# Convolution transfers moved to GpSimd's queue, and gated linear attention slots dealt by product weight

## The reference, cut to what matters

```python
x = layer_norm(x, ln_in_g, ln_in_b)
gq, gk, gv, gr, glow, sq, sk, sv, cb, cc, ch = split_cols(x @ w_in)
go = gated_linear_attention(gq, gk, gv, gr, glow)      # recurrent, blocks of 64 tokens
so = stick_breaking_attention(sq, sk, sv)
co = cb * causal_conv3(cc * ch, conv_w)                # 256 channels
x = layer_norm(ALPHA * x + concat(go, so, co) @ w_out, ln1_g, ln1_b)
x = layer_norm(ALPHA * x + square(relu(x @ w_up)) @ w_down, ln2_g, ln2_b)
```

## Time and profile before

| what | value |
|---|---|
| median of 3 runs | 3136.07 us (3127.56 to 3136.89) |
| the profiled execution: its time, its span | 3133.53 us, 3131.8 us |
| PE busy, DVE busy, ACT busy, POOL busy | 88%, 48%, 34%, 9% of the span |
| mean granted clock of PE | 0.931 |
| `phase_head`, from the span's start to the barrier | 977 us |

### The profile page before, as it was taken

How to read it: one execution, slowest core, us unless ns; L and a number is a source line. 1 busy time by engine, 2 the same in 40 slices (tenths; PEclk the granted TensorE clock), 3 DMA queues, 4 the chain that set the end, 5 groups by cost and what they waited for, 6 DMA issues and landing times. The chain is left out here.

```text
span 3131.8 us, 40707 instructions
## 1 busy us (share of the span) xinstructions
PE 2756.6 (88%) x14670; PEld 2328.9 (74%) x14670; DVE 1501.9 (48%) x2346; ACT 1065.7 (34%) x1768; POOL 266.5 (9%) x285
## 2 busy tenths in 40 slices
PE   5989989899733367999999999999999988999997
PEld 4778787799722355888877888877888866888885
DVE  3446545643433546666556644445644424522224
ACT  1334333333212433444442434443434322322221
POOL 0030020200300001000001100001100000000000
PEclk9989999999855578999999999999999999999998
DMA  4635454343314754666665766665766554545452
GB/s 135 192 117 168 142 165 147 119 126 118 94 30 133 223 165 136 200 214 211 193 209 165 242 193 224 195 206 187 231 206 216 178 174 143 181 157 161 151 172 98
DMA packets 430004, 525.84 MB, mean 168 GB/s; under 512 B 31312, under 2 KB 305152, under 8 KB 429808
## 3 DMA queue, kind: packets, MB, share of 16 engines
q1 hardware_dynamic: 408592, 497.14, 50.2%
q10 hardware_dynamic: 21216, 26.10, 2.4%
HBM read 422.34 MB, written 100.80 MB: 167 GB/s over the span
## 5 line engine op out<-in xcount | busy, mean ns | idle before, releaser
L111 PE MATMUL p_ps_u<-p_xh,p_wh 128*128 128x512 f32 (+1 forms) x1280 | 453.4, 354 | 5.3 <-DVE p_xl L1614 5.3
L112 PE MATMUL p_ps_u<-p_xh,p_wl 128*128 128x512 f32 (+1 forms) x1280 | 451.9, 353 | 0.0
L113 PE MATMUL p_ps_u<-p_xl,p_wh 128*128 128x512 f32 (+1 forms) x1280 | 451.8, 353 | 0.0
L1563 DVE SCALAR_TENSOR_TENSOR p_res<-p_res,p_ps_d 128x512 f32<-128x512 f32 (+1 forms) x340 | 232.1, 685 | 451.4 <-PE p_ps_d L113 445.6
L111 PE MATMUL p_ps_d<-p_wh,p_hh 128*128 128x512 f32 (+1 forms) x1088 | 432.3, 397 | 15.4 <-DVE p_res L1563 13.2
L112 PE MATMUL p_ps_d<-p_wh,p_hl 128*128 128x512 f32 (+1 forms) x1088 | 428.5, 394 | 0.0
L113 PE MATMUL p_ps_d<-p_wl,p_hh 128*128 128x512 f32 (+1 forms) x1088 | 428.2, 394 | 0.0
L1472 ACT ACTIVATE p_wh<-p_wst 128x1024 fp32r<-128x1024 f32 x288 | 294.0, 1049 | 278.8 <-PE p_ps_d L113 219.6
L1621 DVE TENSOR_TENSOR p_r<-p_r 128x512 f32<-128x512 f32 (+1 forms) x160 | 95.8, 599 | 461.4 <-ACT p_hh L1502 461.2
L676 DVE TENSOR_TENSOR p_wl<-p_wst,p_wh 128x1024 fp32r<-128x1024 f32 x96 | 118.0, 1236 | 356.1 <-ACT p_wh L537 355.8
L1495 ACT ACTIVATE p_r<-p_ps_u 128x512 f32<-128x512 f32 (+1 forms) x160 | 83.8, 524 | 578.9 <-PE p_ps_u L113 578.9
(11 more groups left out here) (154 smaller groups left out, 4748.5 us busy)
## 6 DMA issues: line engine op xcount, KB each, us to landing
p_wl<-wlo_scratch SPq DMA_DIRECT2D x216, 512.0 KB, 5.2
p_wst<-in_w_up SPq DMA_DIRECT2D x128, 512.0 KB, 5.8
p_wst<-in_w_down SPq DMA_DIRECT2D x128, 512.0 KB, 5.0
p_wst<-in_w_in SPq DMA_DIRECT2D x96, 512.0 KB, 3.9
wlo_scratch<-p_wl SPq DMA_DIRECT2D x72, 512.0 KB, 3.5
p_kk<-ks_scratch SPq DMA_DIRECT2D x84, 256.0 KB, 5.8
p_vv<-vs_scratch SPq DMA_DIRECT2D x84, 256.0 KB, 4.5
p_wst<-in_w_out SPq DMA_DIRECT2D x32, 512.0 KB, 5.9
```

Of the source, the lines that this page charges most:

```text
L111: pe.matmul(out, lhs_hi, rhs_hi, start=first, stop=False, skip_group_check=skip)
L112: pe.matmul(out, lhs_lo, rhs_hi, start=False, stop=False, skip_group_check=skip)
L113: return pe.matmul(out, lhs_hi, rhs_lo, start=False, stop=last, skip_group_check=skip)
L1563: dve.scalar_tensor_tensor(out=acc, in0=acc, scalar=scale, in1=ps_d[:c, d % DB, :], op0=ALU.mult, op1=ALU.add).then_inc(d_free, 1)
```

## The change

Two things change, both in `phase_head`.

1. The convolution's transfers go from SP to POOL. `c_load` is no more; POOL itself waits for the stores, issues the three loads, does its arithmetic, waits for its own last result and issues the store and the state's transfers.
2. The slots are dealt by weight. From the first F 8 on, an F product counts 2 and a T product 1 (176 in all), and slots are taken so that their number keeps up with 132 times the share of the weight spent, at most two behind one product. Slots are now taken behind T products of all passes. An ahead slot may follow one product behind F 8 as before; a body waits for T pass 1 of its tokens. The two halves of an input normalisation (`norm_a`, `norm_b`) come behind successive F products from F 0 on.

By the new rule, worked from the diff, 16 slots are left for the drain (it begins with "intra 14, gate_sum 8"). Behind these products of the list come two slots: F 13, 15 of the first group; F 4, 6, 8, 10, 12, 14, 16 of the second; F 3, 5, 9, 10, 11, 12, 13, 15 of the third; F 9 to 16 and the first two T products of pass 2 in the last. Behind F 9 of the third and the last group come "load 4, gate 4" and "load 6, gate 6"; behind F 10 gate_sum and decay; behind F 11 level_mul and the first level product.

```diff
@@ the list
-                if step[0] == "F" or step[3] % 2 == 1:
-                    take_slot()
-                ready = [dense_at.get(("F", min(t // 512, 3), conv_f), len(dense_at)) for x, t, cnt in conv]
-                if conv_put < len(conv) and ready[conv_put] + 2 <= len(dense_at):
-                    order += [("c_load", conv_put), ("conv", conv_put)]
+                for n in range(2):
+                    if taken + n < n_slots * spent / sum(weight) and (n == 0 or taken + 1.5 < n_slots * spent / sum(weight)):
+                        taken += take_slot()
+                done.add(("F",) + step[2:4] if step[0] == "F" else ("T",) + step[2:4] if step[4] == len(gtiles[step[2]]) - 1 else None)
+                if conv_put < len(conv) and ("F", min(conv[conv_put][1] // 512, 3), conv_f) in done:
+                    order.append(("conv", conv_put))
...
+        n_slots = sum(len(x) for x in aheads) + 2 * len(bodies[-1]) + NG
+        opens = dense.index([x for x in dense if x[:4] == ("F", 0, 0, gla_f)][0]) + 1
+        weight = [{"F": 2, "T": 1}.get(x[0], 0) if i > opens else 0 for i, x in enumerate(dense)]
...
@@ take_slot
-            if body < NG and ag > body:
+            if b < NG and a > b and ("T", source(b), 1) in done:
...
@@ SP
-                elif what == "c_load":
...
-                elif what == "conv":
...
-                    sp.wait_ge(c_y, 6 * (k + 1))
-                    sp.dma_start(mixt_dram[768 + P * x:768 + P * x + P, t:t + cnt], cin[:, 1, :cnt]).then_inc(c_out, 16)
...
@@ POOL, in its conv step
+                    if x == 0:
+                        wait_stores(pool, results[("F", min(t // 512, 3), conv_f)])
+                    if k:
+                        pool.wait_ge(c_out, 16 * k)
+                    for n, z in enumerate((Z_CC, Z_CH, Z_CB)):
+                        pool.dma_start(cin[:, n, :cnt], zt_dram[z + P * x:z + P * x + P, t:t + cnt]).then_inc(c_in, 16)
...
+                    pool.wait_ge(c_y, 6 * k + 6)
+                    pool.dma_start(mixt_dram[768 + P * x:768 + P * x + P, t:t + cnt], y).then_inc(c_out, 16)
...
+            pool.wait_ge(cs_out, 64)
+            pool.wait_ge(c_out, 16 * len(conv))
```

More of the change, by code:

```diff
@@ L211, in weights, with t_steps @@
             return len(wunits) - 1
-        def t_steps(g, p):
+        def t_steps(sec, g, p):
             u = weights("T", pairs[p], 0)
             weights("T", pairs[p], 1)
[L216 to L230, removed]
-            else:
[L232 to L246, removed]
@@ new lines, in t_steps @@
+            return [("T", sec, g, p, ti, u) for ti in range(len(gtiles[g]))]
+        BOTH = ([0, 1], list(range(len(fs))), [2, 3])
+        sections = [(g, BOTH) for g in range(len(GROUPS))]
+        visits = []
+        for sec, (g, _) in enumerate(sections):
+            again = g in [x for x, _ in sections[:sec]]
+            visits += [dict(sec=sec, t=t, o=o, c=c, again=again) for t, o, c in gtiles[g]]
+        visit_no = {(vt["sec"], vt["t"]): i for i, vt in enumerate(visits)}
+        NORMS = len([vt for vt in visits if not vt["again"]])
@@ new lines, in tiles_of, with prepare @@
+        def tiles_of(sec):
+            return [visit_no[(sec, t)] for t, _, _ in gtiles[sections[sec][0]]]
+        def prepare(i):
+            return [("x_load", i)], [] if visits[i]["again"] else [("norm_a", i), ("norm_b", i)]
+        dense += [("x_load", 0), ("rows",), ("x_load", 1), ("x_load", 2), ("x_load", 3), ("norm_a", 0), ("norm_b", 0)]
+        for sec, (g, (first, middle, final)) in enumerate(sections):
+            more = tiles_of(sec + 1) if sec + 1 < len(sections) else []
+            opening = [t_steps(sec, g, p) for p in first]
+            if sec == 0:
+                for ti, i in enumerate(tiles_of(0)):
+                    if ti + 1 < len(tiles_of(0)):
+                        dense += [("norm_a", i + 1)]
+                    dense += [("turn", i)]
+                    if ti + 1 < len(tiles_of(0)):
+                        dense += [("norm_b", i + 1)]
+                    dense += [steps[ti] for steps in opening]
+            else:
+                for steps in opening:
+                    dense += steps
+            dense += [("x_load", i) for i in more]
+            for n, f in enumerate(middle):
+                dense.append(("F", sec, g, f, None if fs[f][1] == RANK else weights("F", fs[f][0])))
+                for x, i in enumerate(more):
+                    if not visits[i]["again"]:
+                        if n == min(2 * x, len(middle) - 2):
+                            dense.append(("norm_a", i))
+                        elif n == min(2 * x + 1, len(middle) - 1):
+                            dense.append(("norm_b", i))
+            for p in final:
+                for ti, step in enumerate(t_steps(sec, g, p)):
+                    dense.append(step)
+                    if p == final[-1] and 1 <= ti <= len(more):
+                        dense.append(("turn", more[ti - 1]))
+            dense += [("turn", i) for i in more[len(gtiles[g]) - 1:]]
@@ L297, in phase_head @@
         aheads, bodies = [ahead_slots(g) for g in range(NG)], [tile_slots(g) for g in range(NG)]
-        ag = body = 0
-        dense_at, order, next_w, drained = {}, [], 0, False
+        ahead_at = body_at = 0
+        done, order, next_w, drained = set(), [], 0, False
         conv, conv_put = [(x, t, cnt) for t, cnt in GG for x in range(2)], 0
         def take_slot():
-            nonlocal ag, body
-            found, a_before = [], ag
-            if body < NG and ag > body:
[L306 to L314, removed]
+            nonlocal ahead_at, body_at
+            found, a, b = [], ahead_at, body_at
+            if b < NG and a > b and ("T", source(b), 1) in done:
+                found += bodies[b].pop(0)
+                if not bodies[b]:
+                    body_at += 1
+            if a < NG and a <= body_at + 1 and ("F", source(a), gla_f) in done:
+                found += aheads[a].pop(0)
+                if not aheads[a]:
+                    ahead_at += 1
             order.extend(found)
@@ L320, in phase_head @@
             if step[0] == "T":
-                unit_end[step[4]] = unit_end[step[4] + 1] = i
-            elif step[0] == "F" and step[3] is not None:
-                unit_end[step[3]] = i
+                unit_end[step[5]] = unit_end[step[5] + 1] = i
+            elif step[0] == "F" and step[4] is not None:
+                unit_end[step[4]] = i
         def split_weights(i):
@@ L350, in phase_head @@
                     conv_put += 1
-        drained = True
-        while True:
-            took = take_slot()
+        while take_slot() or conv_put < len(conv):
             if conv_put < len(conv):
-                order += [("c_load", conv_put), ("conv", conv_put)]
+                order.append(("conv", conv_put))
                 conv_put += 1
-            elif not took:
-                break
-        assert next_w == len(wunits) and body == NG
+        assert next_w == len(wunits) and body_at == NG
@@ L385, in phase_head @@
                     freed.append((x_lo, n_turn))
-                last_m[("turn", step[1])] = n_turn
+                turned_by[visits[step[1]]["sec"]] = n_turn
             elif step[0] == "gate":
@@ L419, in _ @@
                 if what == "x_load":
[L420 to L425, removed]
+                    i = at[0]
+                    vt, sl = visits[i], i % XS
+                    if i >= XS:
+                        sp.wait_ge(x_hi, 2 * (i - XS + 1))
+                        sp.wait_ge(x_lo, 2 * (i - XS + 1))
+                        sp.wait_ge(xn_out[sl], 16 * len(range(sl, min(i, NORMS), XS)))
+                    t0 = TILES[vt["t"]][0]
+                    if vt["again"]:
+                        sp.wait_ge(xn_out[vt["t"] % XS], 16 * (vt["t"] // XS + 1))
+                    src = xn_dram[t0:t0 + vt["c"], :] if vt["again"] else x_tile(vt["t"])
+                    sp.dma_start(xs[:vt["c"], sl, :], src).then_inc(x_in[sl], 16)
                 elif what == "rows":
@@ new lines, in _ @@
+                    for n, (o, cnt) in enumerate(moving(GROUPS[g][1]) if what == "F" else [(gtiles[g][at[3]][1], 256)]):
+                        q = (i + n) % OUTS
+                        act.wait_ge(m_mm, m + n + 1)
+                        if i + n >= OUTS:
+                            act.wait_ge(out_st[q], 16 * ((i + n) // OUTS))
+                        act.activation(outb[:rows, q, :cnt], ps_m[:rows, (m + n) % DB, :cnt], ACT.Copy).then_inc(m_out, 1)
+                        act.wait_ge(m_out, i + n + 1)
+                        t = GROUPS[g][0] + o
@@ L807, in _ @@
                     u, y, tmp = cu[:, x, :], cin[:, 1, :cnt], cin[:, 0, :cnt]
+                    if x == 0:
[4 more added lines that the diff above has]
+                        pool.dma_start(cin[:, n, :cnt], zt_dram[z + P * x:z + P * x + P, t:t + cnt]).then_inc(c_in, 16)
+                    if t == SEQ:
```

(11 more changed lines are left out.)

119 lines of the change are left out of this document (43 added, 76 removed).

## The result

The changed kernel takes 3214.62 us (median of 4 runs, 3209.38 to 3215.8), the kernel before 3134.91 us (median of 4 as well): a ratio of 1.0255, with a 95% interval of 1.0235 to 1.0276. It is 80 us slower; the forecast had 32 us slower, and a range that ends at 3205. The direction was right and the size wrong.

A forecast was written before the change was run, and what follows sets the result against it. PE standing still or at lower clock was taken as the bound. Head end: 977 - 103 + 22 - 37 = 859, less 30 clock = 829, plus 137 waits and 43 clock = 1009 us; kernel 3168 us, range 3070 to 3205.

The forecast's parts named there:

- the 137 us: Dense stretch of the head: the sum of PE's new waits caused by the new slot list; bounds 37 and 137 x 1.3.
- pairs of level products: Two level products behind one F product: PE waits for DVE's result between them, 42 us with odd leftovers.
- load with gate: Load and gate behind one product: PE waits 9.6 us in GLA groups 4 and 6, 2 in group 2; 21 us.
- chains to the first level product: From gate to first level product in groups 4, 6, 2 and 7: 12.7, 11.5, 10.5 and 9 us; 44 us.
- body pairs: Two body slots behind one product: intra behind gated 4, and three of 2; 10 us.
- v: v_in one product ahead of kv, its load behind the weights' load: 0.8 to 5.7 us, five times; 20 us.
- 58 + 22.6 us and some clock: Transfers to POOL remove PE's drain waits, 9.1 + 48.9 us, and its 22.6 us of waits for weights.
- 859 us, less the clock: Head end without new waits, 37 us of dense waits removed; giving back 30 of 32 us clock loss makes 829.
- the clock on the new waits: Lower PE clock in the dense stretch adds 43 us to the 137 us of new waits; bounds 0 and 103.
- A: Rival: new waits are half those counted; head ends at 918 us, kernel 3077; chance 0.21, its far end 0.06.
- B: Rival: gain and new waits cancel within 9 us, kernel 3136; chance 0.12.
- C: Rival: POOL's chain of convolution pieces ends last in the head; 3195 at 8 us more a piece; chance 0.09.

The follow-up runs named there:

- e1: The kernel before with only the convolution's transfers moved to POOL, its slots dealt as before; 3046.3 us, ratio 0.9704 to the kernel before.
- e3: The changed kernel with at most one slot behind each product; 3109.35 us, ratio 0.9908.
- e5: The changed kernel with the next weights' split (ACT's high half, DVE's low half) behind the product's slots instead of ahead; 3073.5 us, ratio 0.9792.
- e6: The kernel before with the convolution's transfers on POOL and the next weights' split behind the product's slots; 3009.54 us, ratio 0.959.
- the first filling: The changed kernel with 8 to 20 unread products in front of PE's known waits, filling a third to two thirds of each; 3208.62 us.
- the second did not: The changed kernel with more than twice as many unread products, 16 to 42, in front of PE's known waits; 3192.2 us.

## Why the prediction was off

**Right: where the waits would come.** The terms of the 137 us, against the single waits in the trace after: pairs of level products 42 against 41.9; load with gate 21 against 22.9 (4.2, 9.8, 8.8); chains to the first level product 44 against 40.8 (9.0, 11.7, 11.3, 8.8; the last of them is met at `sums`, where PE waits for ACT's `p_sq`, L985, ahead of the level product); body pairs 10 against 11.6; v 20 against 17.2. Sum 134 us. The reading of the earlier trace rows, durations in the order of the list, was sound: each term within some 15%, their sum within 2%.

**Right: the drain.** Fifteen slots left it (31 became 16; the sum had 14 of 30), the 58 us of the earlier trace rows went with SP's steps, and the part from "intra 14" on kept its length. For part 1 alone, my terms (58 + 22.6 us and some clock) give about 95 us; e1 gained 91.

**The step that failed: "859 us, less the clock ... I give back 30. That is 829."** It took all 37 us of the earlier trace rows as removed and then gave 30 us of clock for them. e1 shows what removing really brought in the dense stretch: waits down from 51.1 to 28.0, that is 23 and not 37, and PE busy 707.3 to 694.5, that is 13 and not 30. Only the two kinds that SP or a late ACT had caused went. The waits for v, for the gate's load and for `p_qb` belong to the list, and any list has some of them; the new one has more small ones (nine of 1.5 to 3.4 us, 21 us together) that no term of mine held. So 31 of the 45 us by which the dense stretch exceeded the forecast are in this credit.

**Under-sized: the clock on the new waits.** 43 us forecast. Between e1 and the changed kernel PE is busy 74 us longer, 22 of it the moved product work, so 52 is the clock's, for 142.5 us of waits: 0.36 us for each. Taken with the credit: net +13 us forecast, 39 measured against the kernel before (61 more busy, less 22). My reason for a low price, "a slower PE does not lengthen chains of ACT and DVE", overlooked the products behind the wait, which are PE's own: they run at half speed (2.05 against 1.06 us above). In all kernels of the table that were run without filling, half clock follows the waits at 0.6 to 1.3 us for each, in most of them at 1.1 to 1.2.

**The whole of it.** 180.4 us more of dense stretch = 119.4 waits + 22 moved work + 39 clock; forecast 100 + 22 + 13 = 135. With 2 us of drain and 2 at its start this is the 50 us between 1009 and 1059.

**Also: what the text ahead of the prediction says of the T products is wrong.** It has slots behind each T product of passes 1 and 3. The line is `step[3] % 2 == 1`, and `step[3]` is the tile, not the pass: there is a slot behind every second T product of every pass, so two of them (5.8 us) lie between two slots. The drain has one slot more (31 of 118, with level product 6.7 in front). The list of products with two slots leaves out F 3 of the last group, a body pair before which PE now waits 2.05 us. No term of the sum hung on it, but I overlooked a cost by it: in the new dealing a slot may follow each single T product, 2.9 us of cover. I take that for most of what separates e3 (78 us of waits) from e1 (28), neither with a second slot. It is argued and not isolated, since the positions of the normalisations also differ between these two; 12 of the 50 us are the waits of the turns named above.

**Rivals.** A (half the waits) fails: they came in full. B fails with it. C (POOL last) fails: POOL was done 23 us early. A load's issue takes 0.54 us, 0.74 at most, and a piece 16.6 us ((1034.8 - 951.8) / 5, the stores of pieces 12 and 17) against 15.4 before, so 1.2 us more, where the sum had allowed 3.5. The rule cited for C from the Trainium skill ("SBUF — State Buffer", section "SBUF: two separate sides") makes a GpSimd-issued DMA starve beside certain DVE operations; in 54 issues none shows it here. 29 of them overlap DVE instructions in the trace, mostly float32 tensor_tensor and the masked copy from PSUM, and take 536 to 590 ns, the first 739, against 535 to 567 of the 25 that overlap none. A plain copy on DVE, for which the page gives its 3.1 us, was never among them, so that case stays open.

**Not settled.** The new dealing's chains when `w` is late still hold PE for 20 us at `p_qb` in e5, and I did not run the opening pairs alone. No run moves the normalisations alone, so "add nothing" in the prediction is not shown. Why the first filling left the speed of PE's own work as it was and the second did not stays open beyond their sizes.

## What to carry to other kernels

Where every engine follows one list, ask of each thing that stands ahead of a short chain whether it must: here weights that were needed some products later stood in the way of DVE, ACT and SP, and moving two lines (23 us in the kernel before, 37 with the transfers on POOL, 141 under the new dealing) was worth more than the dealing. Before spreading small work, count what lies between two pieces of it on the engine that waits, and price the waits with their clock. When you credit a wait as removed, name what releases it and whether the edit touches that; otherwise it stays, and so does its share of the clock.

## What was not expected of the hardware

Issuing from POOL was cheap: 54 loads at a median of 540 ns, 18 stores at 598 ns, a store landing a median 2.0 us after its issue. From SP it had been 432 and 320 ns, and 1.7 us. And the clock recovers fully when the waits go: e6 held a mean of 1.00 over 687 us with PE busy 680 of them, where the kernel before held 0.96.
